# Part of three normalizations' product on unnormalized fp32 weights, with two weight chunks interleaved behind them

## The reference

```
def rms_norm(x):       return x * rsqrt(mean(x * x) + 1e-6)
def adaln(x, mod, k):  return rms_norm(x) * (1 + mod[k + 1]) + mod[k]
def swiglu(h, w_in, w_out):
    g, u = split(h @ w_in, 2);  return (silu(g) * u) @ w_out

for layer in (0, 1):
    h = h + 0.5 * mod[2] * swiglu(adaln(h, mod, 0), ffn_in[layer, 0], ffn_out[layer, 0])
    a = adaln(h, mod, 3)
    y = hyena_mixer(a, ...) if layer == 0 else mamba2_mixer(a, ...)   # begins with a @ in_w
    h = h + mod[5] * y
    h = h + 0.5 * mod[8] * swiglu(adaln(h, mod, 6), ffn_in[layer, 1], ffn_out[layer, 1])
return rms_norm(h) * final_norm_w
```

## Time and profile before

| | |
|---|---|
| time, median of 3 runs | 1992.54 us (1991.73 to 1992.66) |
| the profiled execution's own time | 1992.9 us |
| its span, first to last instruction | 1991.1 us |
| PE busy | 1953.2 us, 98% |
| DVE busy | 1286.4 us, 65% |
| ACT busy | 719.1 us, 36% |
| mean granted TensorE clock | 0.994 of full |

### The profile page before, as it was taken

The page is one execution under the profiler, slowest core; times in us unless marked ns, Lnnn a source line. Parts: engine busy times, 40 slices in busy tenths (PEclk is TensorE's granted clock), DMA queues, the critical chain, the costliest instruction groups (busy, mean ns, idle before and its releaser), DMA issues. The chain is left out here.

```text
span 1991.1 us, 24598 instructions
## 1 busy us (share of the span) xinstructions
PE 1953.2 (98%) x9953; PEld 1632.0 (82%) x9953; DVE 1286.4 (65%) x1793; ACT 719.1 (36%) x1015; POOL 212.1 (11%) x151
## 2 busy tenths in 40 slices
PE   7999999999999999999999999999999998999998
PEld 4788888878888878888888888888888896698898
DVE  5755546678788575654777655557676578956654
ACT  4522222242311342222324222222344545735553
POOL 1000000100065300000110000001000003540001
PEclk9999999999999999999999999999999999999999
DMA  9544335533440253442654444245443345744554
GB/s 372 198 152 148 128 113 172 174 136 124 170 164 1 85 189 128 158 138 74 208 167 146 167 148 148 88 172 169 162 148 112 114 147 169 238 151 167 190 179 139
DMA packets 65861, 306.45 MB, mean 154 GB/s; under 512 B 9395, under 2 KB 10068, under 8 KB 46550
## 3 DMA queue, kind: packets, MB, share of 16 engines
q1 hardware_dynamic: 61670, 293.05, 42.7%
q10 hardware_dynamic: 4080, 11.85, 1.6%
HBM read 298.44 MB, written 6.43 MB: 153 GB/s over the span
## 5 line engine op out<-in xcount | busy, mean ns | idle before, releaser
L1771 PE MATMUL banks<-xhl,wh 128*128 128x512 f32 (+1 forms) x1756 | 664.9, 379 | 7.0 <-DVE xhl L1136 2.7
L1772 PE MATMUL banks<-xhl,wh 128*128 128x512 f32 (+1 forms) x1756 | 662.0, 377 | 0.0
L1773 PE MATMUL banks<-xhl,wl 128*128 128x512 f32 (+1 forms) x1756 | 661.9, 377 | 0.0
L1056 DVE TENSOR_TENSOR wl<-raw,wh 128x2048 fp32r<-128x2048 f32 (+2 forms) x193 | 398.7, 2066 | 230.1 <-ACT wh L607 224.9
L607 ACT ACTIVATE wh<-raw 128x2048 fp32r<-128x2048 f32 (+1 forms) x200 | 347.3, 1736 | 530.8 <-PE banks L1773 486.1
L1771 PEld LDWEIGHTS banks<-xhl,wh 128*128 128x128 f32 x1756 | 330.9, 188 | 75.3 <-DVE xhl L1136 6.5
L1773 PEld LDWEIGHTS banks<-xhl,wl 128*128 128x128 f32 x1756 | 330.9, 188 | 60.8
L1772 PEld LDWEIGHTS banks<-xhl,wh 128*128 128x128 f32 x1756 | 330.9, 188 | 59.4
L1771 PE MATMUL banks<-gh,wh 128*128 128x512 f32 (+1 forms) x704 | 255.3, 363 | 0.0
L1772 PE MATMUL banks<-gl,wh 128*128 128x512 f32 (+1 forms) x704 | 255.2, 362 | 0.0
L1773 PE MATMUL banks<-gh,wl 128*128 128x512 f32 (+1 forms) x704 | 255.2, 362 | 0.0
(11 more groups left out here) (282 smaller groups left out, 2071.8 us busy)
## 6 DMA issues: line engine op xcount, KB each, us to landing
raw<-in_ffn_in SPq DMA_DIRECT2D x88, 1024.0 KB, 4.8
raw<-in_ffn_out SPq DMA_DIRECT2D x64, 704.0 KB, 4.2
ada_rawf<-in_ada_rest SPq DMA_DIRECT2D x60, 512.0 KB, 3.5
ada_rawo<-in_ada_rest SPq DMA_DIRECT2D x48, 512.0 KB, 3.5
raw<-in_mb_in_w SPq DMA_DIRECT2D x24, 1024.0 KB, 4.8
raw<-in_hy_in_w SPq DMA_DIRECT2D x12, 1024.0 KB, 4.9
afb<-decays SPq DMA_DIRECT2D x32, 256.0 KB, 4.6
raw<-in_mb_out_w SPq DMA_DIRECT2D x8, 1024.0 KB, 4.8
```

Source lines behind the costliest of these rows:

```text
L1056: dve.tensor_tensor(wl[n_slot][:, 0:cols], raw[r_slot][:, 0:cols], wh[n_slot][:, 0:cols].bitcast(F32), ALU.subtract).then_inc(w_lo, 1)
L1771: pe.matmul(dst, h, x_hi, start=start, stop=False)
L1772: pe.matmul(dst, h, x_lo, start=False, stop=False)
L1773: return pe.matmul(dst, l_, x_hi, start=False, stop=stop)
```

## The change

It touches the norms "hy", "10" and "mb" and the first two chunks behind them.

For the latent half of channel tiles 0 to 3 (RAW_K = 4) the product with chunk 0 is no longer made from the split, normalized activations. PE multiplies xs, not yet normalized, by the raw fp32 weights in eight matmuls of 257 columns (raw_products) into banks 6 and 4; the 257th column holds the shift mod[k]. These matmuls stand where the unread ones stood: one between the two groups of sums, two before the spread of 1/rms, five behind it. ACT copies both results into pp; at the end of the norm DVE multiplies them by 1/rms and, when chunk 0 is used up, adds them and the shift's column to banks 0 and 1 (mix). ACT reads banks 0 and 1 only after that (semaphore mixed). Tile 0 is now normalized context half first.

first_pair_mixed takes the place of first_pair in the three stages: for each channel tile, chunk 0 and then the high part of chunk 1 (ahead: four matmuls of 512 columns); after the last tile the low part of chunk 1 for all tiles (16 matmuls). SyncE loads chunk 2 into the raw buffer only after the raw products, and ACT writes xh of tiles 0 to 3 only after those of the tile. xs gets a layout of 513 columns a tile for the first four tiles.

```diff
+            def raw_products(key, w, i0, i1):
+                for i in range(i0, i1):
+                    k, s = i // 2, i % 2
+                    if s == 0:
+                        pe.wait_ge(xs_done, SCALED[key] * DT + k + 1)
+                    ins = pe.matmul(raw_bank(s)[:, 0:L + 1], raw[w.raw % 2][:, k * 256 + s * P:k * 256 + s * P + P],
+                                    xs[:, k * (NT + 1):k * (NT + 1) + L + 1], start=k == 0, stop=k == RAW_K - 1)
+                    if s:
+                        ins.then_inc(raw_mm, 1)
...
             def norm(key, w=None, n=NT):
+                if key in SCALED:
+                    pe.wait_ge(w_hi, w.w + 1)
+                    norm_sums(key, n, lambda: raw_products(key, w, 0, 1))
+                    raw_products(key, w, 1, 3)
+                    norm_spread(key, n)
+                    raw_products(key, w, 3, 2 * RAW_K)
+                    return
...
+            def first_pair_mixed(pl, q, halves):
+                first, second = pl.w % 2, (pl.w + 1) % 2
+                def ahead(k):
+                    for s in range(2):
+                        h_ = wh[second][:, k * 256 + s * P:k * 256 + s * P + P]
+                        pe.matmul(bank[2 + s][:], h_, xh[:, k, :], start=k == 0, stop=False)
+                        pe.matmul(bank[2 + s][:], h_, xl[:, k, :], start=False, stop=False)
+                pe.wait_ge(w_lo, pl.w + 1)
+                for k in range(DT):
+                    pe.wait_ge(*((p_lo, q + k + 1) if k else (lo_lat, halves)))
+                    toks = (slice(L, NT),) if k < RAW_K else (slice(0, L), slice(L, NT)) if k == RAW_K else (slice(0, NT),)
+                    for s in range(2):
+                        for tok in toks:
+                            ins = mm3(bank[s][:, tok], first, k * 256 + s * P, xh[:, k, tok], xl[:, k, tok], k == 0, k == DT - 1)
+                    if k == 0:
+                        pe.wait_ge(p_lo, q + 1)
+                        pe.wait_ge(w_hi, pl.w + 2)
+                    if k < DT - 1:
+                        ahead(k)
+                ins.then_inc(w_used, 1)
+                ahead(DT - 1)
+                pe.wait_ge(w_lo, pl.w + 2)
+                for k in range(DT):
+                    for s in range(2):
+                        ins = pe.matmul(bank[2 + s][:], wl[second][:, k * 256 + s * P:k * 256 + s * P + P], xh[:, k, :],
+                                        start=False, stop=k == DT - 1)
+                ins.then_inc(w_used, 1)
...
+                def mix():
+                    dve.wait_ge(raw_out, 2 * SCALED[key] + 2)
+                    for s in range(2):
+                        own.mark(dve.tensor_tensor(pp[s][:, 0:L], pp[s][:, 0:L], bank[7][:, 0:L], ALU.mult))
+                    own.sync()
+                    dve.wait_ge(w_used, w.w + 1)
+                    for s in range(2):
+                        ins = dve.scalar_tensor_tensor(bank[s][:, 0:L], pp[s][:, 0:L], pp[s][:, L:L + 1],
+                                                       bank[s][:, 0:L], ALU.add, ALU.add)
+                    ins.then_inc(mixed, 1)
...
                 second_lo()
+                if key in SCALED:
+                    mix()
...
+                    if key in SCALED and k < RAW_K:
+                        act.wait_ge(raw_mm, SCALED[key] * RAW_K + k + 1)
...
+                    if key in SCALED and k in (RAW_K, RAW_K + 1):
+                        s = k - RAW_K
+                        act.activation(pp[s][:, 0:L + 1], raw_bank(s)[:, 0:L + 1], ACT.Copy).then_inc(raw_out, 1)
```

## The result

The changed kernel takes 2036.06 us (median of 5 runs, 2035.73 to 2037.65), the kernel before 1992.54 us beside it: ratio 1.0218, interval 1.0207 to 1.0229. It is 43.5 us slower, where 6.4 us slower was forecast and 1993.5 to 2003 given as the range. The direction was right, the size wrong by a factor of seven, and the time lies outside the range.

A forecast was written before the change was run, and what follows sets the result against it. PE, 98% busy, bounds the kernel, but DVE bounds "hy". Chunk 2's +4.2 - 1.1 - 0.4 = +2.7, plus clock 2.0 + 1.7, gives +6.4: 1998.9 us on the median's scale; own range 1996.5 to 2001.5, wider range 1993.5 to 2003.

The forecast's parts named there:

- The small things: ACT's copies, SyncE's later load of chunk 2, ACT's new waits: a tenth either way, nothing booked.
- the signs that the prediction named for being right: "hy": ada_weigh near 450, 8 us wait, then clock 0.50; "10", "mb": 2 us waits; second chunk ends 3 us earlier.
- Removal and interleaving: Three stages: 24 matmuls fewer, 2.8 us; tile 1 to chunk 0's end takes 13.1 us against 9.79, 3.3 later.
- The +0.15 us of the raw products: In the norm, tile 1 ready 0.15 us later; bounded by 0 and, at half clock, +1.1.
- Mix: DVE behind chunk 0: multiplications free, two additions 0.9 us (0.7 to 1.3), plus 0.1 for handing over.
- Chunk 2: PE waits 8, 1.9 and 2.6 us in "hy", "10", "mb"; 4.2 us lost, 1.1 and 0.4 gained.
- The clock: Half-clock stretches after new waits: +2.0 us in "hy", +1.7 for one of "10" and "mb"; ends 0 and +3.4.
- the prediction's 8.1 us: The total slowdown if all three new waits for chunk 2 brought a clock fall, instead of 6.4 us.
- The sum without layout: Whole kernel: 2.7 us from chunk 2 plus 2.0 and 1.7 from the clock, +6.4 us.
- The rivals: Clock stays up, near 1995.2 us (0.22); saved work decides, 1983.5 (0.08); half clock in norms too, 2003.5 (0.12).
- B: Rival: chunk 2 ready in time everywhere, each stage gains 3.0 us, 1983.5 us in all; chance 0.08.
- B's own point of decision: In "hy", a chain whose ada_weigh runs before mix: from there the saved work would decide, 1983.5 us; chance 0.08.

The follow-up runs named there:

- e5: The whole change with 512 bytes instead of 64 between xh and xl: 2001.41 us, ratio 1.0046 to the kernel before.
- e1: The kernel before with only the changed memory layout, 64 bytes between xh and xl: 2024.9 us, ratio 1.0167.
- e4: The whole change with 128 bytes instead of 64 between xh and xl: 2011.58 us, ratio 1.0100 to the kernel before.
- e10: e5 with chunk 1 interleaved with tiles 0 to 3 only: 1993.52 us, ratio 0.9999 to the kernel before.
- e9: e10 with ACT's high part of chunk 2 before the wait for mixed in "hy" and "10", and "hy" low parts one step earlier: 1983.33 us.
- e11: The kernel before with 256 bytes between xh and xl, nothing else changed: 1994.17 us, ratio 0.9998.
- e12: The kernel before with 64 free bytes ahead of xh, so all of PE's operands move together: 1994.21 us, ratio 1.0004.
- e14: The kernel before with 32 bytes behind xl, so all weight slots lie 32 bytes further from xh and xl: 2024.27 us, ratio 1.0151.
- e2: The kernel before with 64 bytes behind xl; xh and xl stay, everything behind them moves: 2023.15 us, ratio 1.0149.
- e13: The kernel before with only the wl slots and what lies behind them moved by 64 bytes: 2015.56 us, ratio 1.0107.

## Why the prediction failed, point by point

*The small things.* The step that failed is "nothing is booked" for what the change does beside its instructions. The list there had ACT's copies and SyncE's load; the 64 bytes between xh and xl were part of the same diff and were not weighed at all. They carry 34.5 of the 42.8 us of span (e5 against the changed kernel), and 32 us alone (e1). The trace of before could not have priced them, since the operands of these matmuls all lie at multiples of 512 bytes from one another; but a change of addresses that may touch each of 4464 matmuls should have stood among the rivals, with its size called unknown. All the signs that the prediction named for being right did come (ada_weigh behind the additions, the waits, the low clock, chunk 0 over 3 us later), and the total was wrong by 37 us all the same, because every sign lay in the three stages that the change was about.

*Removal and interleaving.* Right in mechanism and size. Forecast 13.1 us from tile 1 to the end of chunk 0; e5, without the layout, has 434.95 to 448.23, which is 13.3. The +0.15 us of the raw products was 0: tile 1 starts 7.8 us behind the first sum in both. A raw product cost 0.433 us and not 0.445: ten records begin 0.217 us apart. In the earlier trace rows the 16 records begin within 3.46 us (1657.71 to 1661.17), 0.216 each; the 3.56 of the prediction holds one interval too many. For five products that is 0.06 us.

*Mix.* Right: 0.88 us, with ACT's read behind it.

*Chunk 2.* Waits forecast 8, 1.9 and 2.6 us; measured 8.0, 3.1 and 2.6 in e5, and 7.9, 3.0 and 2.4 after. The 1.1 us missing in "10" can be seen in the timelines of ACT and DVE, before and then after:
```profile
1078.71 1.28 ACT L682 ACT_TABLE_LOAD   x1
1081.65 1.09 ACT L682 ACTIVATE tt<-banks 128x512 f32<-128x512 f32 x2 [1.65 <-PE banks L1773]
```
```profile
1112.64 0.88 DVE L1179 SCALAR_TENSOR_TENSOR banks<-pp,banks 128x256 f32<-128x256 f32 x2 [2.86 <-PE banks L1820]
...
1113.62 1.28 ACT L707 ACT_TABLE_LOAD   x1 [7.62 <-DVE banks L1179]
1114.92 1.08 ACT L707 ACTIVATE tt<-banks 128x512 f32<-128x512 f32 x2
...
1117.83 2.29 DVE L1087 TENSOR_TENSOR wl<-raw,wh 128x2048 fp32r<-128x2048 f32 x1 [4.31 <-ACT wh L625]
```
The load of ACT's table for this function takes 1.28 us. Before, it stood ahead of the wait for chunk 0 and was over 1.65 us before the banks were ready; with the added wait for mixed it began only when mixed had come, and so stood on the chain. The chain was read off, which begins behind the load, so it was missing from the sum. That the added wait moved it is read from these two timelines; no run tried it otherwise.

*The clock.* Right in kind. Behind the 8 us wait the granted clock was low; windows of the kernel after around the restarts in "hy" and "10" (A:B length, PE busy, PEclk, DMA share, GB/s):
```profile
468.90:474.80 5.90, 5.90 (x15) 0.55 0.53 181
1119.30:1126.90 7.60, 6.72 (x17) 0.55 0.33 78
```
Both windows hold a little more than the stretch: PE ran at 0.50 from 468.9 to 474.3 and from 1120.1 to 1126.2. These 5.4 and 6.0 us are longer than the 3.5 to 4.1 of the earlier trace rows; they lost about 2.7 and 3.0 us, forecast 2.0 and 1.7. In e5 the stretches were in "hy" and "mb" and none in "10", though its wait was the longer of the two. One of the two short waits was booked and one came, in both kernels; that is partly luck, since in e4, with waits of 3.0 and 2.5 us, neither brought a fall. The norms' own stretches in "10" and "mb" were gone in the kernel after and in e5. The Trainium skill, "TensorE: Matmul & The Clock Gate", section "HAM oscillation — how this bites in real kernels", warns of waits between groups of matmuls, and it ties this to their length. The long wait in "hy" (5.3 to 8.0 us in the kernel after, e4, e5 and e10) agrees each time. For waits of 2.4 to 3.1 us there was a fall in one of two in the kernel after, one of two in e5 and none of two in e4, so taking the page's warning for all three waits, as the prediction's 8.1 us did, would have been too much.

*The sum without layout.* Forecast +6.4 us, the span of e5 is 8.3 us longer than before: "hy" +5.8 (forecast 6.2), "10" +0.4 (-1.1), "mb" +2.3 (+1.3 with the clock), the rest about 0. Of the 1.9 us between sum and span the table load explains 1.1; the last us, in "mb", was not traced.

*The rivals.* None of the rivals was the one that happened; none spoke of the layout. B had priced the saved work at 3 us a stage and 1983.5 us in all, and e9 measured 1983.33. But B's own point of decision, ada_weigh ahead of mix, was not tried: in e9 ada_weigh still stands behind mix, and what changed is that the low part of chunk 2 goes ahead of it, ACT's high part does not wait for mixed, and half of the interleaving is taken back.

## What to carry to other kernels

A change of an address is a change of the kernel: when a buffer gets padding, list every operand behind it that PE streams or loads as weights, and keep activations and weights apart by a multiple of 256 bytes (here 32 and 64 bytes cost 1.5 to 1.7%, 128 about a third of that, 256 and 512 nothing; no other distances were tried). Stages whose instructions are the same in both kernels are the first thing to compare; a difference there says that the cause is not in the part that was changed on purpose. And when work is moved to let one engine run ahead, ask when the shared slot behind it comes free: interleave only as far as the pacing engine makes PE wait.

## What the runs showed of the hardware

The time from start to start of fp32r matmuls of 512 columns depends on the distance in SBUF between activations and weights. It is 0.227 us for each of the three of mm3 where all distances are multiples of 256 bytes (before, e5, e11, e12). It is 0.233 us with the weights 32 or 64 bytes off from xh and xl (e14, e2), 0.235, 0.238 and 0.230 with 64 bytes between xh and the rest (e1, after), and 0.232, 0.226 and 0.228 with 128 bytes there (e4). For 256 columns no cost was seen. Moving all of these operands by 64 bytes made no difference. Which pair of operands decides for one matmul stays open, and so does the reason.

The Trainium skill, "TensorE: Matmul & The Clock Gate", section "Step-by-step: what each phase is for", says that streaming and the loading of the next weights have read ports of their own and that the loading does not take bandwidth from the running matmul. By that one would not expect the place of the weights to matter. In e13, where only the place of wl changed, the matmul on wl went from 0.227 to 0.236 us, and the measurement decides. That both reads meet at some shared part of the memory would be a guess, which no run here tests.
